# A streaming encoder's setup stage: where its small matmuls, row loads and bias expansion stand

## What is computed

```python
def ada_norm(x, c, w, b, g):
    m = jax.nn.silu(c) @ w + b                       # c: 9 conditioning rows; w: 1024 x 3072
    shift, scale, gate = jnp.split(m[:, None, :], 3, axis=-1)
    return rmsnorm(x, g) * (1 + scale) + shift, gate
...
for l in range(DEPTH):                               # layer 0: differential + windowed attention, layer 1: relative-bias band
    hp, gp = ada_norm(xp, c_prompt, ada_w[l, 0], ada_b[l, 0], norm_g[l, 0])
    ...                                              # attention, xp = xp + gp * yp
    hp, gp = ada_norm(xp, c_prompt, ada_w[l, 1], ada_b[l, 1], norm_g[l, 1])
    ...                                              # conv-FFN, xp = xp + gp * fp
```

## Time and profile before

| | us |
|---|---|
| median of 3 runs | 3787.69 |
| lowest and highest run | 3777.33, 3791.2 |
| the profiled execution's own time | 3792.35 |
| span of the profiled execution | 3790.8 |
| mean granted TensorE clock, share of full | 0.948 |
| PE busy | 3449.8 (91%) |
| DVE busy | 2121.2 (56%) |
| ACT busy | 1344.2 (35%) |
| bytes moved | 303.87 MB, mean 80 GB/s |

### The profile page before, as it was taken

One profiled execution on the slowest core, in us unless ns is written; L12 is line 12 of the kernel. 1 busy time (PEld: TensorE's weight loads), 2 busy tenths in 40 slices (PEclk: granted clock), 3 DMA queues, 4 the chain that ended last, 5 costly groups with the idle time before them and its releaser, 6 DMA issues. The chain is left out here.

```text
span 3790.8 us, 54306 instructions
## 1 busy us (share of the span) xinstructions
PE 3449.8 (91%) x20953; PEld 2039.6 (54%) x20953; DVE 2121.2 (56%) x3554; ACT 1344.2 (35%) x2665; POOL 479.5 (13%) x1018
## 2 busy tenths in 40 slices
PE   6978888685989999999989898899798999999998
PEld 3545555453655555555555555555465555555555
DVE  5665555554465555555565555555456555555555
ACT  5744555443232122212234444545332222122221
POOL 1012332221100000000001122222210000000000
PEclk8889999897989999999989999999898999999998
DMA  9723232123111111111022333333521111111111
GB/s 346 267 78 96 68 92 81 54 71 105 37 51 40 40 45 40 44 40 45 29 70 65 114 121 117 125 125 125 182 62 34 46 43 38 49 40 39 40 45 56
DMA packets 222127, 303.87 MB, mean 80 GB/s; under 512 B 24339, under 2 KB 174151, under 8 KB 221314
## 3 DMA queue, kind: packets, MB, share of 16 engines
q1 hardware_dynamic: 191938, 190.39, 15.4%
q0 software_dynamic: 30016, 111.15, 9.6%
HBM read 264.76 MB, written 63.95 MB: 87 GB/s over the span
## 5 line engine op out<-in xcount | busy, mean ns | idle before, releaser
L96 PE MATMUL psum<-h,ffn_high 128*128 128x512 f32 (+1 forms) x2016 | 986.6, 530 | 2.8 <-ACT u L890 2.8
L98 PE MATMUL psum<-hl,ffn_high 128*128 128x512 bf16 (+1 forms) x2016 | 614.7, 338 | 0.0
L100 PE MATMUL psum<-h,ffn_low 128*128 128x512 bf16 (+1 forms) x2016 | 561.6, 332 | 0.0
L96 PE MATMUL psum<-actr,ffn_high 128*128 128x512 f32 (+1 forms) x960 | 472.4, 532 | 7.3 <-DVE xT L604 7.3
L96 PEld LDWEIGHTS psum<-h,ffn_high 128*128 128x128 f32 x2016 | 389.5, 193 | 82.2 <-ACT u L890 3.0
L98 PEld LDWEIGHTS psum<-hl,ffn_high 128*128 128x128 bf16 x2016 | 196.5, 97 | 411.4 <-issue 355.2
L86 PE MATMUL psum<-h,attC_high 128*128 128x384 f32 x744 | 353.5, 475 | 33.0 <-DMA hl<-act_low_dram 14.8
L950 DVE TENSOR_SCALAR y<-u,cvT 128x1168 f32<-128x1168 f32 x88 | 78.1, 888 | 516.1 <-ACT u L895 515.9
L86 PE MATMUL psum<-h,attAB_high 128*128 128x384 f32 x648 | 312.0, 482 | 27.4 <-DMA hl<-act_low_dram 12.8
L98 PE MATMUL psum<-actl,ffn_high 128*128 128x512 bf16 (+1 forms) x960 | 295.2, 341 | 0.0
L182 ACT CAST ffn_high<-ffn_raw 128x1024 fp32r<-128x1024 f32 x130 | 137.2, 1055 | 397.5 <-PE psum L100 388.3
(11 more groups left out here) (514 smaller groups left out, 7262.3 us busy)
## 6 DMA issues: line engine op xcount, KB each, us to landing
ada_raw<-in_ada_w SPq DMA_DIRECT2D x48, 1024.0 KB, 8.4
ffn_raw<-in_w_up SPq DMA_DIRECT2D x88, 512.0 KB, 3.7
ffn_raw<-in_w_down SPq DMA_DIRECT2D x44, 512.0 KB, 3.5
raw_C<-in_cache_c_k POOLq DMA_DIRECT2D x64, 256.0 KB, 4.3
raw_C<-in_cache_c_v POOLq DMA_DIRECT2D x64, 256.0 KB, 3.4
out_ck_s<-in_cache_c_k POOLq DMA_DIRECT2D x8, 1984.0 KB, 9.0
out_cv_s<-in_cache_c_v POOLq DMA_DIRECT2D x8, 1984.0 KB, 14.5
attC_raw<-in_w_in_odd SPq DMA_DIRECT2D x24, 512.0 KB, 5.3
```

What stands on the lines that cost most here:

```text
L96: return pe.matmul(out, w, x[:, lo:hi], start=first and start, stop=last and stop, skip_group_check=True)
L98: return pe.matmul(out, top(w), xl[:, lo:hi], start=first and start, stop=last and stop, skip_group_check=True)
L100: return pe.matmul(out, wl, top(x[:, lo:hi]), start=first and start, stop=last and stop, skip_group_check=True)
```

## The change

In `setup`:

- The columns are computed by thirds: the 8 column matmuls of unit u - 1 stand in unit u, two behind each of its last four steps k; the last third stands behind unit 11. All four bias rows are loaded at once beside `msb`, and the selecting constant has four versions of ten columns, so POOL's reloads go. The result banks of the units are swapped (even units 2 and 3, odd units 0 and 1), and the small transposes of unit 1 use bank 6.
- The five x row loads stand ahead of chunks 6, 12, 20, 28 and 36 instead of all ahead of chunk 6.
- The diagonal and the spread of the first norm are made in unit 11: DVE behind its last split, PE behind step k = 5.
- The expansion of the bias to 2 MB goes to the head of layer 0's `ffn` on SP, ahead of its weight loads, and the mask write to the end of that block's weight loads; `setup` only writes the row table and the mask tile to DRAM.

```diff
-        for t in range(0, QB, 2):
-            sp.dma_start(xrow[:, t:t + 2, :], ins["x_prompt"][0, t * P:(t + 2) * P, :].rearrange("(t p) d -> p t d", p=P)
-                         ).then_inc(S.x_in[t // 2], 16)
-        sp.dma_start(xrow[:, QB, :], ins["x_sample"].rearrange("b t d -> (b t) d")).then_inc(S.x_in[QB // 2], 16)
         for c in range(6, FBASE):
+            if c in X_AT:                            # X_AT = (6, 12, 20, 28, 36)
+                x_rows(X_AT.index(c))
             chunk(c)
...
-            if a and j == 0:
-                act.wait_ge(S.mod_mm, a)
+            if a:
+                act.wait_ge(S.mod_mm, u - 2)
             act.copy(msb[0:2 * NC9, j * D:(j + 1) * D],
...
+        def columns(u, part):
+            a, j = units[u]
+            if part == 0:
+                pe.wait_ge(S.ada_evac, u + 1)
+                pe.wait_ge(S.adab_in, 16)
+                if a and j == 0:
+                    pe.wait_ge(S.mod_evac, a)
+            for n in range(8 * j + 2 * part, 8 * j + 2 * part + 2):
+                mm = pe.matmul(ps[:, 7, 10 * n:10 * n + 10], msb[0:2 * NC9 + 4, n * P:(n + 1) * P],
+                               K[0:2 * NC9 + 4, C_ADA + 10 * a:C_ADA + 10 * a + 10], start=(n == 0), stop=(n == 23),
...
                 if k % 2:
                     mm.then_inc(S.f_used[c % 3], 1)
+                if u and k >= 4:
+                    columns(u - 1, k - 4)
+                if u == 11 and k == 5:
+                    pe.wait_ge(S.ada_evac, 11)
+                    pe.wait_ge(S.x_evac, 18)
+                    pe.wait_ge(S.set_ones, 3)
+                    spread_pe(pe, S, G, 0, diag, *G.spread)
...
-            if a and j == 0:
-                columns(a - 1)
-        columns(3)
+        for part in range(4):
+            columns(11, part)
...
         def modulation(a):
-            dve.wait_ge(S.mod_mm, a + 1)
+            dve.wait_ge(S.mod_mm, 3 * a + 3)
...
-                if u == 11 and k == 2:
+                if u == 11 and k == 0:
                     rstd_dve(dve, S, G, 0)
+                    diag_dve(dve, S, G, 0, diag)
...
+            if l == 0:
+                sp.dma_start(G.bias_dram, bass.AP(G.rev_dram.tensor, P - 1, [[384, 16], [-1, P], [1, 256]])
+                             ).then_inc(S.rev_out, 16)
             groups(sp, body)
+            if l == 0:
+                sp.wait_ge(S.rev_out, 48)
+                sp.dma_start(G.bias_dram[:, 0:CHUNK, 256 - CHUNK:256].rearrange("h i j -> i h j"),
+                             G.neg_dram.unsqueeze(1).broadcast_to([CHUNK, 16, CHUNK])).then_inc(S.rev_out, 16)
+                sp.wait_ge(S.rev_out, 64)
```

More of the change, by code:

```diff
@@ L43 @@
 C_ADA = C_CA + 64
-C_SEL = C_ADA + 10
+C_SEL = C_ADA + 40
 C_L = C_SEL + 2
@@ L59, in shape_constants @@
     for b in range(NC9):
-        c[b, C_ADA + b] = c[NC9 + b, C_ADA + b] = c[2 * NC9, C_ADA + b] = 1
+        for a in range(4):
+            n = C_ADA + 10 * a + b
+            c[b, n] = c[NC9 + b, n] = c[2 * NC9 + a, n] = 1
     c[0, C_L:C_L + CHUNK] = 1
@@ L242, in setup, with unit_bank @@
     turns = [range(max(0, 2 * u - 2), min(18, 2 * u)) for u in range(len(units))]
+    def unit_bank(u):
+        return 2 - 2 * (u % 2)
     def x_bank(q):
@@ L252, in chunk, with x_rows @@
             ring.load(sp, c, ada_w[a, j, k], view=("p (k n) -> p k n", dict(k=2)))
+        def x_rows(i):
+            if 2 * i < QB:
+                sp.dma_start(xrow[:, 2 * i:2 * i + 2, :],
+                             ins["x_prompt"][0, 2 * i * P:(2 * i + 2) * P, :].rearrange("(t p) d -> p t d", p=P)
+                             ).then_inc(S.x_in[i], 16)
+            else:
+                sp.dma_start(xrow[:, QB, :], ins["x_sample"].rearrange("b t d -> (b t) d")).then_inc(S.x_in[i], 16)
         sp.dma_start(crow[0:1, :], ins["c_prompt"]).then_inc(S.c_in, 16)
@@ L284, in _ @@
         pool.memset(G.mhalf[:, :], -0.5).then_inc(S.set_ones, 1)
-        pool.dma_start(msb[2 * NC9:2 * NC9 + 1, :], ada_b[0:1, :]).then_inc(S.adab_in, 16)
+        pool.dma_start(msb[2 * NC9:2 * NC9 + 4, :], ada_b[0:4, :]).then_inc(S.adab_in, 16)
         pool.dma_start(vrow[0:32, :], ins["norm_g"].rearrange("l s (k p) -> (l s k) p", p=P)).then_inc(S.vec_in, 16)
@@ L361, in turn @@
             mm.then_inc(S.x_turned, 1)
[L363 to L369, removed]
+        def columns(u, part):
[8 more added lines that the diff above has]
+                               K[0:2 * NC9 + 4, C_ADA + 10 * a:C_ADA + 10 * a + 10], start=(n == 0), stop=(n == 23),
                                skip_group_check=True)
-            mm.then_inc(S.mod_mm, 1)
+            if part == 3:
+                mm.then_inc(S.mod_mm, 1)
         for u, (a, j) in enumerate(units):
@@ L380, in _ @@
                     cols = slice(D * (k % 2) + 512 * h, D * (k % 2) + 512 * (h + 1))
-                    pe.matmul(ps[:, 2 * (u % 2) + h, :], cst[:, k, :], w[:, cols], start=(k == 0), stop=False)
-                    mm = pe.matmul(ps[:, 2 * (u % 2) + h, :], cb[:, k, :], wl[:, cols],
+                    pe.matmul(ps[:, unit_bank(u) + h, :], cst[:, k, :], w[:, cols], start=(k == 0), stop=False)
+                    mm = pe.matmul(ps[:, unit_bank(u) + h, :], cb[:, k, :], wl[:, cols],
                                    start=False, stop=(k == KT - 1))
@@ L542, in mod_act, with diag_dve @@
             act.copy(G.h[:, :, SEQ:TOK], ts[:, 0:KT * TS].rearrange("p (k t) -> p k t", k=KT)).then_inc(S.hs_high, 1)
+def diag_dve(dve, S, G, m, diag):
+    dve.wait_ge(S.rstd9, m + 1)
+    d3, ident = diag[:, 0:TOK].rearrange("p (t d) -> p t d", d=P), G.consts[:, C_ID:C_ID + P]
+    for lo, hi in ((0, 4), (4, TB)):
+        dve.tensor_tensor(d3[:, lo:hi, :], ident.unsqueeze(1).broadcast_to([P, hi - lo, P]),
+                          G.rstd9[:, lo:hi].unsqueeze(2).broadcast_to([P, hi - lo, P]), ALU.mult).then_inc(S.diag, 1)
 def mod_dve(dve, ch, S, G, m, tmp, diag, ts, rs, rs_s, ring, c):
@@ L551, in mod_dve @@
         rstd_dve(dve, S, G, m)
[L552 to L556, removed]
+        diag_dve(dve, S, G, m, diag)
     dve.wait_ge(S.root, m + 1)
@@ L1176, in attention @@
         m = 2 if odd else 0
-        rs, rs_s = ps[:, 3:5, :].rearrange("p b n -> p (b n)"), ps[:, 7, TS:2 * TS]
+        rs, rs_s = (ps[:, 3:5, :].rearrange("p b n -> p (b n)"), ps[:, 7, TS:2 * TS]) if odd else G.spread
         sq = [F["q"][:, :], F["k"][:, :], F["v"][:, :], E[:, 0:TOK], sw[:, :]]
@@ L1551, in _ @@
         def _(pe):
-            spread_pe(pe, S, G, m, F["v"], rs, rs_s)
+            if odd:
+                spread_pe(pe, S, G, m, F["v"], rs, rs_s)
             def do(what, kind, T, s, c, turns):
@@ L2342, in encoder @@
         G.psum = ctx.enter_context(nc.psum_tensor("psum", [P, 8, 512], F32))
+        G.spread = (G.psum[:, 3:5, :].rearrange("p b n -> p (b n)"), G.psum[:, 2, 0:TS])
+        G.neg_dram = nc.dram_tensor("neg_dram", (CHUNK, CHUNK), F32, kind="Internal").ap()
         G.rev_dram = nc.dram_tensor("rev_dram", (16, 384), F32, kind="Internal").ap()
```

21 lines of the change are left out of this document (8 added, 13 removed).

## The result

The changed kernel takes 3811.3 us, median of 4 runs (3809.5 to 3815.7), against 3787.2 for the kernel before in runs beside it; the ratio is 1.0068, with an interval of 1.0052 to 1.0085. Run again beside seven runs of before it took 3812.1 against 3784.2, ratio 1.0076 (1.0049 to 1.0103). It is 24 to 28 us slower, 0.7 to 0.8%. The forecast was 3777.2, with a range of 3762 to 3790: 10 us faster, counted as no difference. The sign was wrong, and the time lies above the range.

What follows compares the result with a forecast made beforehand. ACT was taken to bound undisturbed setup units (10.24 us), PE everything behind setup. The terms, -7.6 - 25.2 + 19.5 - 1.1 - 1.1 + 5.0 = -10.5 us, took the median from 3787.69 to 3777.2, range 3762 to 3790.

Steps and rivals of the forecast that it cites:

- X rows: Setup, chunk 6: with x row loads spread, it lands at 29.1 instead of 38.02 us; gain 7.6 us.
- Columns out of their blocks: Setup: threading column matmuls into the units removes 25.2 us of blocks; what is added in their place taken at nothing.
- an alternative at 0.5 us: Setup: if columns and weight matmuls don't overlap as well, 0.5 us in each of 8 units.
- The wait for the modulation: Setup, third chunk of three units: PE waits 4.8 us for DVE's modulation, then half clock; 6.5 us lost each, 19.5.
- about 4 us: Setup: length of PE work put at half clock behind each gap for the modulation.
- as long as the old blocks: Setup: upper end of the loss by the modulation wait, 25.2 us; as a rival 3787 us in all, chance 0.15.
- The rival of a clock that stays low: Setup: with pairs in every unit PE's clock might not come back; eight units lose 57 us, 3834; chance 0.08.
- Half clock during the old blocks: Setup before: PE goes to half clock during a block's small matmuls; ACT takes 18.95 and 17.74 us instead of 10.24.
- End of setup: From the end of the last split to setup's end: 10.6 us instead of 11.8; gain 1.1 us.
- Head of the first attention: First attention: DVE no longer waits for the spread, the stall moves to the second weight chunk; gain 1.1 us.
- Bias expansion: Head of layer 0's ffn: the expansion stands ahead of the first weights in the same queue; loss 5 us, between 4 and 6.
- the rival of shared engines: Head of layer 0's ffn: weight loads share the engines with the expansion; 5 us less, 3772; chance 0.13.

Runs made afterwards that it cites:

- a_modfirst: Changed kernel with DVE making the modulation at the start of the next modulation's second unit, ahead of that unit's first split; 3776.2 us, ratio 0.9970 to the kernel before.
- a_bias_behind: Changed kernel with only the 2 MB bias expansion moved behind the loads of the first group of layer 0's ffn; 3798.8 us, ratio 1.0031 to the kernel before.
- fourth profile of before: The kernel before, unchanged, profiled a fourth time; its profiled execution took 3791.7 us.
- a_block8: As a_modfirst, with a unit's eight column matmuls in one piece behind step k = 5 instead of four pairs; 3773.0 us, ratio 0.9969 to the kernel before.
- a_best2: As a_block8, with the bias expansion behind the loads of the ffn's first group; 3759.9 us, ratio 0.9933 to the kernel before.
- a_modk0: Changed kernel with DVE's modulation behind the first split of the unit instead of the second; 3799.2 us, ratio 1.0039 to the kernel before.

## Why the prediction was wrong, step by step

- **X rows**: right. -7.6 expected; 8.4 to 9 us in profiles of the kernel with nothing else changed, 7.6 in medians. In the changed kernel the split of chunk 10 came at 43.5, not 40.4. The first third of columns stands in chunks 6 and 7, behind the gap of 2.99 us for chunk 6, and the half clock there lasted from 35.3 to 49.3, 14 us, more than the sum had allowed for.
- **Columns out of their blocks**: the 25.2 us removed fit the rest of the sum (no run takes out the blocks alone), but what was put in their place was not free. The step took the cost of a column matmul inside a block (0.22 us) for its cost between wide matmuls. A pair took 0.73 us there at full clock, 2.9 us a unit instead of 1.7, and PE became the bound: 11.2 to 11.5 us a unit, about 1 us for each unit without a gap. This was named as an alternative at 0.5 us and taken at nothing, without a row that shows a column matmul between wide ones.
- **The wait for the modulation**: the place, the cause and the gap (4.8 expected, 4.85 measured) were right, and a_modfirst shows that it decides the sign. The size was wrong: 19.5 us expected, 3 x 11.3, 11.4 and 10.6 over an undisturbed unit of before, so 33. This is the step that failed. The sum took "about 4 us" of half clock behind the gap and names no row for it; the nearest is 159.55, 4.05 us of weight matmuls behind a block, not behind a gap. Behind the gap of 2.48 us, with weight matmuls and turns, the trace of before had half clock for 6.1 us, from 68.92 to 75.0. With pairs among the weights it lasted 12.9 to 13.1 us. Even the upper end, "as long as the old blocks" (25.2), was too low by 8 us. The rival of a clock that stays low had the mechanism, but as a state of all units; it held in the three units with a gap, and in unit 1, which has the gap of chunk 6.
- **Half clock during the old blocks**: the sum read the slow chunks behind a block as the block's doing. In the unit from 145.78 that is so: 1.00 in the first 4 us of its block and 0.50 behind it. In the first of the three units the clock had already fallen at the gap before the block, came back in it at about 75 and fell a second time at about 78.6.
- **End of setup**: -1.1 expected, -2.0 measured. PE waits 0.33 us for the diagonal, and the spread runs at full clock (1.96 us for its wide part instead of 3.46).
- **Head of the first attention**: -1.1 expected, -1.2 measured, with the wait on the second weight chunk as described.
- **Bias expansion**: 5 us expected, 7.4 to 8.0 measured. The place in the queue was the right mechanism, as a_bias_behind shows. The landing time was taken from a transfer with nothing behind it (9.1 us); with weight loads queued behind, it landed after 12.2 (12.2 to 12.8 in five more profiles, 9.1 and 9.4 in two with nothing behind it) and the first cast began 13.9 us behind the issue, instead of at the 10.5 of the sum. Whether the loads behind take part of the engines meanwhile, which would mix in a little of the rival of shared engines, no run separates.
- **The sum**: with the measured sizes it reads -9 - 25 + 33 + 7 (the plain units) + 3 (unit 1) - 2 - 1.2 + 8 = +13.8, beside 16.2 between the profiled executions. The 2.4 us between them are not accounted for. The range was too narrow above because the two added costs, stall and pairs, were bounded one at a time, while they feed each other: the pairs lengthen the half clock that the gap starts.

The Trainium skill (TensorE: Matmul & The Clock Gate, HAM oscillation) was used for the rule that each gap is paid twice. The trace bears that out for the gaps of 4.85 us, and more strongly than the sum had it: in unit 4 the loss is 11.3, of which 4.85 are the gap, about 1 is what pairs cost in any unit and the rest half clock. For a short gap it doesn't always hold: the 2.48 us in the fourth profile of before were paid once.

## What to carry to other kernels

When a step is split and threaded between others, look for each wait that it had at its old place, and where its signal stands in the other engine's program: here one line of DVE two splits too late turned a gain of 10 us into a loss of 24. Price a small matmul by a row in which it stands between large ones, and never add a gap and small matmuls as if they were independent. A bulk transfer without a reader nearby belongs behind the loads that a block starts with, not ahead of them.

## What the runs showed of the hardware

- The clock of PE, once down to 0.50 behind a gap of 4.85 us, stayed there for 12.9 to 13.1 us while pairs of 10-column matmuls stood between the 512-column ones, in each of three units, and for 7 to 9.6 us with the same eight in one piece (gaps of 3.84 to 4.55 us). The same pairs without a gap left it at 1.00 for whole units of 11.18 us. The same eight in one piece, also without a gap, were followed by half clock in some units of a_block8 (86.1 to 90 us) and in none of the six from 83.7 to 146.2 us in a_best2.
- A gap of 2.57 us with pairs behind it was followed by half clock in each of three units of a_modk0. One of 2.48 us was followed by it in the first profile of before and not in the fourth (1.00 in the stretch from 66.50).
- A pair of 22-row, 10-column fp32 matmuls took 0.73 us between wide matmuls at full clock. Eight in one piece took 1.95 us, 0.24 each.
- A 2 MB DRAM to DRAM transfer landed 9.1 us behind its issue with nothing queued behind it, and 12.2 us with weight loads queued behind it.
